# A three-layer transformer block on one core: the start, the order of the products of rows_wide, and some orders beside them

## The chip, the cores and the metric

The kernel runs on one core of a Trainium2 chip. The metric is the device time of one execution in microseconds (us). Five engines work side by side, each through its own list of instructions: TensorE (PE in the profile, its weight loads PEld), VectorE (DVE), ScalarE (ACT), GpSimd (POOL) and SyncE (SP), which here only starts transfers. They wait for each other by semaphores: `then_inc` raises one when an instruction is done, `wait_ge` holds an engine until it has a value.

## The reference, cut to what matters

Two blocks over 256 tokens of 1024 features, all in float32.

```
first_block(x, mem):
    h = rms_norm(x, g_mix);  proj = h @ w_in          # conv, sq, sk, sv, xq, three gates
    y_conv, y_sb (stick-breaking attention), y_x (attention on rms_norm(mem) @ w_mem_kv)
    merged = gate0 * y_conv + gate1 * y_sb + gate2 * y_x
    x = x + merged @ w_out
    x = x + square(relu(rms_norm(x, g_mlp) @ w_up)) @ w_down
second_block(x), two layers:
    proj = x @ w_in;  fox attention (8 heads) and retention (4 heads, rotary q and k)
    x = layernorm(alpha * x + mixed @ w_out)
    x = layernorm(alpha * x + square(relu(x @ w_ff1)) @ w_ff2)
```

## The kernel before, in words

**Products.** A float32 product is made of three products of rounded parts (type fp32r): high weights by high operand, low weights by high operand, high weights by low operand. The high part is a rounded copy that ScalarE makes, the low part is what is left of the float32 value, by VectorE. Weights come in halves of 128 x 2048 numbers (1 MB). For each half SP loads `raw` (two slots), ScalarE's `split` (L347) copies the high part to `w_hi`, VectorE's `split` (L824) puts the low part into `w_lo` (rings of four slots each), and TensorE takes the half when `lo_ready` has counted it. SP's load of a half waits until VectorE has split the half that used the slot before.

**Three ways over a half.** `rows_part` (L1479) has weights stationary and 256 tokens moving: products of 256 columns, called narrow here. `tokens_part` (L1532, L1533, L1540) has tokens stationary and 512 weight columns moving: wide products, first the four pairs with high operand, then the four with low operand. `rows_wide` (L1516, L1518), used for 14 halves in each of three feed-forward networks (`ffn`), has weights stationary and moves the high and low operand together (512 columns) under the high weights, then the high operand alone (256) under the low weights; for each of two groups `nt` it goes over eight `k`, and the two products of a `k` follow each other.

**The start.** The first two halves come in eight pieces of 512 columns. SP starts x (transposed, four pieces of 256 KB) and the eight pieces of weights by turns on its one queue. In `front_piece` ScalarE multiplies x by the gain (L569) and copies the weights' high part (L572), VectorE makes both low parts (L1137, L1143), and `front_half` on TensorE (L1732 to L1734) takes a piece when its low weights are there. Then ScalarE squares x, VectorE adds the squares (L852, L854), TensorE sums them over partitions (L1743, L1586), and from the variance come a logarithm and an exponential on ScalarE (L367, L369) and a Newton step on VectorE (L838 to L842). With this root `values_out` (L578) scales the products of halves 0 and 1, then of 2 and 3, out of PSUM, and `rms_tile` (L872), `rms_hi` (L383) and `rms_lo` (L878) make the normed operand. The orders of ScalarE and VectorE over these steps and the splits of halves 2 to 7 are written out by hand; they are in the diff. TensorE takes halves 2 and 3 with `tokens_part`, 4 and 5 with `rows_first` on the gained x, and from 6 on the normed operand, of which it waits for one quarter after the other. Half 5 needs the bank that values_out(1) reads.

**The merged half.** Before the product with `w_out` (halves WO1 = 60 to 63) the sum of the gated branches is turned by TensorE (`turn_merged`, L1566) into PSUM banks `turned(m, j)` of `aps`, copied by ScalarE (L651) and its low part made by VectorE (L1240). The banks of `j` = 1 are those that half 61 accumulates in, so half 61 waits until the low part of `j` = 1 is made (the `c = m + 3`).

**mlp_norm** adds the residual (L904), squares (L405 on ScalarE), takes the root and scales (L930, four chunks); TensorE turns a chunk (L1558, `turn`), ScalarE copies it (`turn_hi`, L390), VectorE makes the low part (`turn_lo`, L896). **The layers:** `rotate` (L1360 to L1366) turns q and k of the retention in four steps, which TensorE then transposes (`turn_rotated`, L1879). **ffn** goes in a loop of three rounds (`Fori`) over up (two halves of `rows_wide`), down (two halves of `tokens_part` for both blocks of 128 tokens), up, down; `last_down` takes the last two halves, block 0 of the tokens first. Then `layer_norm` adds (L906), takes statistics (L955) and ends in the stores of the output.

## Time and profile before

| | us |
|---|---|
| median of 3 runs (1213.28 to 1213.96) | 1213.61 |
| the profiled execution | 1213.38 |
| its span, first to last instruction | 1211.6 |

The rows of the trace that the prediction rests on stand in a section of their own. In them times are us from the span's start unless marked ns. A timeline row is: start, duration, engine, line, operation, what it writes <- what it reads, shapes, and in brackets the engine's idle time ahead of it with what ended it; `x2` means that like neighbours are merged. L12 is line 12 of the kernel before. A queue's rows end in q (SPq). Matmuls are pipelined: one row's end lies behind the next row's start, and the distance of two starts is the pace. A plain float32 product is counted as two.

### The profile page before, as it was taken

How to read it: one execution, taken by the hardware profiler on the slowest of the kernel's cores; microseconds unless marked ns; L12 is line 12 of the kernel's file. 1: busy time of each engine (PE TensorE's matmuls, PEld its weight loads, DVE VectorE, ACT ScalarE, POOL GpSimd, SP SyncE). 2: the span in 40 equal slices, each digit the busy share in tenths (PEclk: the TensorE clock that was granted, in tenths of full speed). 3: DMA queues.
4: the chain of work that ended last, by engine and by line, in shares of the span. 5: the costliest groups of instructions: out<-in, count | busy, mean ns of one | idle time of the engine just before them, and what ended most of it. 6: DMA issues, size and time to landing. Idle time of an engine off the chain costs nothing.

```text
span 1211.6 us, 16483 instructions
## 1 busy us (share of the span) xinstructions
PE 1192.4 (98%) x6488; PEld 1012.0 (84%) x6488; DVE 802.4 (66%) x951; ACT 616.2 (51%) x769; POOL 3.5 (0%) x10
## 2 busy tenths in 40 slices
PE   7999999999999999999999999999999999999997
PEld 6999988888888788888888878888878878888885
DVE  5687986564656576656368686665686768766555
ACT  6577675564445455344356545443536554544441
POOL 0000000000000000000000000000000000000000
PEclk9999999999999999999999999999999999999999
DMA  7565354543554365555264446555536444655540
GB/s 254 210 209 174 117 189 151 208 172 139 221 206 177 113 235 200 182 202 179 104 243 174 148 175 219 203 201 179 195 113 249 169 148 174 206 211 175 206 173 35
DMA packets 34488, 219.22 MB, mean 181 GB/s; under 512 B 4080, under 2 KB 6144, under 8 KB 9088
## 3 DMA queue, kind: packets, MB, share of 16 engines
q1 hardware_dynamic: 33792, 216.31, 50.4%
q0 software_dynamic: 640, 2.11, 0.5%
q8 instruction: 41, 0.67, 0.2%
q14 instruction: 15, 0.12, 0.0%
HBM read 217.34 MB, written 1.06 MB: 180 GB/s over the span
## 4 chain that ended last, share of the span: by engine, by line
PE 92%; DVE 6%; ACT 1%; issue 1%; DMA 0%; SPq 0%; DVEq 0%; ACTq 0%
PE gps L1479 13%; PE gps L1516 13%; PE gps L1532 9%; PE gps L1540 9%; PE gps L1533 9%; PE aps L1532 8%; PE aps L1533 8%; PE aps L1540 8%; PE gps L1518 7%; DVE w_lo L824 1%; PE aps L1558 1%; DVE rs L955 1%; ACT w_hi L347 1%; DVE B L965 1%; PE aps L1695 1%
## 5 line engine op out<-in xcount | busy, mean ns | idle before, releaser
L824 DVE TENSOR_TENSOR w_lo<-raw,w_hi 128x2048 fp32r<-128x2048 f32 x194 | 444.2, 2291 | 240.2 <-ACT w_hi L347 239.3
L347 ACT ACTIVATE w_hi<-raw 128x2048 fp32r<-128x2048 f32 x194 | 371.4, 1915 | 211.8 <-PE aps L1540 106.3
L1516 PE MATMUL gps<-R_both,w_hi 128*128 128x512 f32 x672 | 238.1, 399 | 0.0
L1518 PE MATMUL gps<-R_both,w_lo 128*128 128x256 f32 x672 | 188.8, 281 | 0.0
L1532 PE MATMUL aps<-w_hi,Q_hi 128*128 128x512 f32 x416 | 162.7, 391 | 0.5 <-DVE Q_lo L1240 0.5
L1533 PE MATMUL aps<-w_lo,Q_hi 128*128 128x512 f32 x416 | 162.5, 391 | 0.0
L1516 PEld LDWEIGHTS gps<-R_both,w_hi 128*128 128x128 f32 x672 | 126.4, 188 | 30.8
L1518 PEld LDWEIGHTS gps<-R_both,w_lo 128*128 128x128 f32 x672 | 127.1, 189 | 0.8
L1532 PE MATMUL gps<-w_hi,H_hi 128*128 128x512 f32 x288 | 114.9, 399 | 0.0
L1533 PE MATMUL gps<-w_lo,H_hi 128*128 128x512 f32 x288 | 112.6, 391 | 0.0
L1540 PE MATMUL aps<-w_hi,Q_lo 128*128 128x512 f32 x416 | 111.7, 391 | 0.0
L1479 PE MATMUL gps<-H_hi,w_hi 128*128 128x256 f32 x416 | 110.0, 287 | 0.0
L1479 PE MATMUL gps<-H_hi,w_lo 128*128 128x256 f32 x416 | 108.5, 283 | 0.0
L1532 PEld LDWEIGHTS aps<-w_hi,Q_hi 128*128 128x128 f32 x416 | 78.1, 188 | 17.4 <-DVE w_lo L824 0.7
L1540 PEld LDWEIGHTS aps<-w_hi,Q_lo 128*128 128x128 f32 x416 | 77.9, 188 | 16.4
L1533 PEld LDWEIGHTS aps<-w_lo,Q_hi 128*128 128x128 f32 x416 | 78.2, 188 | 15.7
L1479 PE MATMUL gps<-H_lo,w_hi 128*128 128x256 f32 x416 | 83.2, 283 | 0.0
L1479 PEld LDWEIGHTS gps<-H_hi,w_hi 128*128 128x128 f32 x416 | 79.6, 191 | 3.1 <-issue 3.0
L435 ACT ACTIVATE staged<-gps 128x256 f32<-128x256 f32 x84 | 27.6, 381 | 105.6 <-PE gps L1518 105.6
L1479 PEld LDWEIGHTS gps<-H_hi,w_lo 128*128 128x128 f32 x416 | 79.8, 192 | 0.1
L1540 PE MATMUL gps<-w_hi,H_lo 128*128 128x512 f32 x288 | 77.7, 392 | 0.0
L1532 PEld LDWEIGHTS gps<-w_hi,H_hi 128*128 128x128 f32 x288 | 54.1, 188 | 14.3 <-issue 3.5
(239 smaller groups left out, 1562.8 us busy)
## 6 DMA issues: line engine op xcount, KB each, us to landing
raw<-w SPq DMA_DIRECT2D x194, 1024.0 KB, 4.8
B<-rows SPq DMA_DIRECT2D x4, 1024.0 KB, 4.7
raw<-w SPq DMA_DIRECT2D x8, 256.0 KB, 5.7
B<-turns POOLq DMA_DIRECT2D x4, 512.0 KB, 4.6
B<-x_t SPq DMA_DIRECT2D x4, 256.0 KB, 5.3
B<-mem_t SPq DMA_DIRECT2D x1, 1024.0 KB, 8.8
B<-x SPq DMA_DIRECT2D x1, 1024.0 KB, 6.8
out<-B SPq DMA_DIRECT2D x4, 256.0 KB, 2.0
```

The source lines that it names most:

```text
L347: act.activation(w_hi[:, ring(l), :], raw[:, raw_slot(l), :], ACT.Copy)\
L435: act.activation(staged[:, a, nt * T:(nt + 1) * T], wide_bank(a, nt)[:, T:2 * T], ACT.Copy)\
L824: dve.tensor_tensor(w_lo[:, ring(l), :], raw[:, raw_slot(l), :], w_hi[:, ring(l), :].bitcast(F32), ALU.subtract)\
L955: st.mark(dve.bn_stats(stats[:, m, 6 * j:6 * j + 6], chunk(X, m, j)))
L965: dve.scalar_tensor_tensor(t, t, stats[:, m, 17:18], b_row[:, 512 * j:512 * (j + 1)], ALU.mult, ALU.add).then_inc(s["t_z"], 1)
L1479: return pe.matmul(gps[:, bank_, nt * T:(nt + 1) * T], w[:, r, c:c + P], op[:, k, :], start=start, stop=stop, skip_group_check=True)
L1516: pe.matmul(b, w_hi[:, r, c:c + P], R_both[:, k, :, :].rearrange("p i t -> p (i t)"), start=(k == 0), stop=False, skip_group_check=True)
L1518: ins = pe.matmul(b[:, 0:T], w_lo[:, r, c:c + P], R_hi[:, k, :], start=False, stop=(k == KT - 1), skip_group_check=True)
L1532: pe.matmul(out, x, w_hi[:, r, c], start=(start and k == ks[0]), stop=False)
L1533: pe.matmul(out, x, w_lo[:, r, c], start=False, stop=False)
L1540: ins = pe.matmul(out, op_lo[:, 4 * g + k, rows], w_hi[:, r, c], start=False, stop=(stop and k == ks[-1]))
L1558: ins = pe.transpose(turned(m, j)[:, k * P:(k + 1) * P], chunk(src, m, j)[:, k * P:(k + 1) * P], ident)
```

## The change

x goes through ScalarE's DMA queue, ahead of its table load, and SP starts weights alone. TensorE begins with six products of zeros, behind a memset on VectorE. `front_half` takes the high weights with both parts of x first and the low weights last, with finer waits. The orders of ScalarE and VectorE in the start, in mlp_norm and around `rotate(3)` are changed. `rows_wide` makes the eight wide products of a group first, then the eight narrow ones. The merged half's `j` = 1 is turned into banks 3 and 0 of `gps`, half 61 waits for `m + 1` alone, and ScalarE's table load there moves behind the copies. In the last ffn the loop has two rounds, the third is written out, and its last four halves go over block 0 of the tokens first, then block 1.

```diff
@@ -161,7 +161,7 @@
         raw_loaded = [sem("raw_loaded0"), sem("raw_loaded1")]
         x_piece = [sem(f"x_piece{i}") for i in range(4)]
         w_piece = [sem(f"w_piece{i}") for i in range(8)]
-        names = """qk_scaled front_g front_hi front_lo vs_var vs_log vs_scale mem_loaded x_loaded par_loaded cst_loaded con_loaded lpar_loaded out_stored
+        names = """zeros front_xlo qk_scaled front_g front_hi front_lo vs_var vs_log vs_scale mem_loaded x_loaded par_loaded cst_loaded con_loaded lpar_loaded out_stored
             hi_ready lo_ready gemm_done evac act_step dve_step pads
             nsq nsum nvar nlog nrow nt nhi nlo resid acc_ready sqsum rows_loaded gn_row_loaded
             t_sq t_var t_log t_z t_tr
@@ -201,6 +201,10 @@

             return aps[:, 2 * m + j, :]

+        def merged_turned(m, j):
+
+            return turned(m, 0) if j == 0 else (gps[:, 3, :], gps[:, 0, :])[m]
+
         def operand(buf, m, j):

             return buf[:, 4 * j:4 * j + 4, m * P:(m + 1) * P]
@@ -258,9 +262,6 @@

             sp.dma_start(par[:, :], par1).then_inc(s["par_loaded"], 16)
             for k in range(KT):
-                if k % 2 == 0:
-                    sp.dma_start(B6[:, k:k + 2, :], x_t[k * P:(k + 2) * P].rearrange("(k p) t -> p k t", p=P))\
-                      .then_inc(x_piece[k // 2], 16)
                 c = slice(k % 4 * 512, k % 4 * 512 + 512)
                 sp.dma_start(raw[:, raw_slot(k // 4), c], w1[k // 4][:, c]).then_inc(w_piece[k], 16)
             sp.dma_start(cst[:, :], con1).then_inc(s["cst_loaded"], 16)
@@ -410,9 +411,9 @@
                 root_start(0, 0)
                 turn_hi(N_MLP, 0, R_hi)
                 squared(1, 0)
-                turn_hi(N_MLP, 1, R_hi)
                 squared(1, 1)
                 root_start(0, 1)
+                turn_hi(N_MLP, 1, R_hi)
                 split(0, FFN1 + 2)
                 turn_hi(N_MLP, 2, R_hi)
                 turn_hi(N_MLP, 3, R_hi)
@@ -561,6 +562,9 @@
                                    bias=small[:, 1, 2 * h + t:2 * h + t + 1], scale=1.0 / 16,
                                    accum_out=small[:, 2, 2 * h + t:2 * h + t + 1]).then_inc(s["cx_exp"], 1)

+            for k in range(0, KT, 2):
+                act.dma_start(B6[:, k:k + 2, :], x_t[k * P:(k + 2) * P].rearrange("(k p) t -> p k t", p=P))\
+                   .then_inc(x_piece[k // 2], 16)
             act.preload_act_table_set("natural_log_exp_and_others")
             def front_piece(k):
                 c = slice(k % 4 * 512, k % 4 * 512 + 512)
@@ -592,13 +596,13 @@
             values_out(0)
             rms_hi(0, 0, B4, H_hi)
             split(0, 4)
+            split(0, 5)
+            values_out(1)
             rms_hi(0, 1, B4, H_hi)
-            split(0, 5)
             rms_hi(0, 2, B4, H_hi)
-            values_out(1)
             split(0, 6)
+            split(0, 7)
             rms_hi(0, 3, B4, H_hi)
-            split(0, 7)
             staged_n = 0
             for h in range(SQK, FFN1):
                 ps = bank(h)
@@ -642,14 +646,14 @@
                             act.wait_ge(s["staged_free"], staged_n - 1)
                             evac(staged[:, m, :], bank(h - 1 + m), h + 1)
                             staged_n += 1
-                elif h == WO1:
-                    act.preload_act_table_set("natural_log_exp_and_others")
                 if h in (GATED["conv"] + 4, WO1):
                     for m in range(2):
                         j = int(h == WO1)
                         act.wait_ge(s["mg_tr"], 2 * j + m + 1)
-                        act.activation(operand(Q_hi, m, j), four(turned(m, j)), ACT.Copy)\
+                        act.activation(operand(Q_hi, m, j), four(merged_turned(m, j)), ACT.Copy)\
                            .then_inc(s["mg_hi"], 1)
+                if h == WO1:
+                    act.preload_act_table_set("natural_log_exp_and_others")
                 if h == MEM0:

                     act.wait_ge(s["mem_loaded"], 16)
@@ -926,20 +930,25 @@
                                       EPS_RMS, ALU.add, ALU.add).then_inc(s["t_var"], 1)
                     dve.wait_ge(s["t_var"], m + 1)
                     root(0, m)
-                    for j in range(2):
-                        dve.scalar_tensor_tensor(chunk(scaled, m, j), chunk(X, m, j), stats[:, m, 17:18],
-                                                 g_mlp[:, 512 * j:512 * (j + 1)], ALU.mult, ALU.mult)\
-                           .then_inc(s["t_z"], 1)
+
+                def scaled_chunk(m, j):
+                    dve.scalar_tensor_tensor(chunk(scaled, m, j), chunk(X, m, j), stats[:, m, 17:18],
+                                             g_mlp[:, 512 * j:512 * (j + 1)], ALU.mult, ALU.mult)\
+                       .then_inc(s["t_z"], 1)

                 added(0, 0)
                 added(0, 1)
                 dve.wait_ge(s["rows_loaded"], 16)
                 rooted(0)
+                scaled_chunk(0, 0)
+                scaled_chunk(0, 1)
                 added(1, 0)
                 turn_lo(N_MLP, 0, R_hi, R_lo)
                 added(1, 1)
+                rooted(1)
+                scaled_chunk(1, 0)
                 turn_lo(N_MLP, 1, R_hi, R_lo)
-                rooted(1)
+                scaled_chunk(1, 1)
                 turn_lo(N_MLP, 2, R_hi, R_lo)
                 split(0, FFN1 + 2)
                 turn_lo(N_MLP, 3, R_hi, R_lo)
@@ -1135,7 +1144,8 @@
                 c = slice(k % 4 * 512, k % 4 * 512 + 512)
                 dve.wait_ge(s["front_g"], k + 1)
                 dve.scalar_tensor_tensor(Q_lo[:, k, :], B6[:, k, :], par[:, G_MIX + k:G_MIX + k + 1],
-                                         Q_hi[:, k, :].bitcast(F32), ALU.mult, ALU.subtract)
+                                         Q_hi[:, k, :].bitcast(F32), ALU.mult, ALU.subtract)\
+                   .then_inc(s["front_xlo"], 1)
                 if k % 4 == 3:
                     dve.wait_ge(s["hi_ready"], k // 4 + 1)
                 else:
@@ -1144,6 +1154,7 @@
                                   ALU.subtract).then_inc(s["lo_ready" if k % 4 == 3 else "front_lo"], 1)

             g_mix, g_mem = (par[:, g:g + KT] for g in (G_MIX, G_MEM))
+            dve.memset(staged[:, 0, 0:T], 0.0).then_inc(s["zeros"], 1)
             dve.wait_ge(s["par_loaded"], 16)
             for k in range(KT):
                 front_piece(k)
@@ -1169,9 +1180,9 @@
             rms_root(0)
             rms_tile(0, B6, B4, g_mix)
             split(0, 4)
+            split(0, 5)
             rms_tile(1, B6, B4, g_mix)
             rms_lo(0, 0, B4, H_hi, H_lo)
-            split(0, 5)
             rms_tile(2, B6, B4, g_mix)
             rms_lo(0, 1, B4, H_hi, H_lo)
             scaled_half(0)
@@ -1237,7 +1248,7 @@
                     for m in range(2):
                         j = int(h == WO1)
                         dve.wait_ge(s["mg_hi"], 2 * j + m + 1)
-                        dve.tensor_tensor(operand(Q_lo, m, j), four(turned(m, j)),
+                        dve.tensor_tensor(operand(Q_lo, m, j), four(merged_turned(m, j)),
                                           operand(Q_hi, m, j).bitcast(F32), ALU.subtract)\
                            .then_inc(s["mg_lo"], 1)
                 if h == MEM0:
@@ -1399,10 +1410,10 @@
                     if l == 12:
                         for h in range(RET_HEADS):
                             retention_mask(h)
+                    if l == 10:
+                        rotate(3)
                     if l <= LRV:
                         split(g0, p + l + 4)
-                    if l == 10:
-                        rotate(3)
                     if l == 12:
                         dve.wait_ge(s["gn_row_loaded"], 16 * (ly + 1))
                         scaled_gate(0)
@@ -1515,6 +1526,8 @@
                         c = k * 256 + nt * P
                         pe.matmul(b, w_hi[:, r, c:c + P], R_both[:, k, :, :].rearrange("p i t -> p (i t)"),
                                   start=(k == 0), stop=False, skip_group_check=True)
+                    for k in range(KT):
+                        c = k * 256 + nt * P
                         ins = pe.matmul(b[:, 0:T], w_lo[:, r, c:c + P], R_hi[:, k, :],
                                         start=False, stop=(k == KT - 1), skip_group_check=True)
                 ins.then_inc(s["gemm_done"], 1)
@@ -1563,7 +1576,7 @@

                 pe.wait_ge(s["mg"], 2 * j + m + 1)
                 for k in range(4):
-                    ins = pe.transpose(turned(m, j)[:, k * P:(k + 1) * P],
+                    ins = pe.transpose(merged_turned(m, j)[:, k * P:(k + 1) * P],
                                        chunk(merged, m, j)[:, k * P:(k + 1) * P], ident)
                 ins.then_inc(s["mg_tr"], 1)

@@ -1627,13 +1640,29 @@
                     ins.then_inc(s["up_tr"], 1)
                 rows_wide(h0, l0 + 3, 1)
                 down(h0, l0 + 4, 0, ub + 2, first=True)
-                with pe.Fori(0, 3) as f:
+                with pe.Fori(0, 3 if n < LAYERS else 2) as f:
                     hf, uf = h0 + f * 8, ub + f * 4
                     up(hf, l0 + 6, uf + 3)
                     down(hf, l0 + 8, 1, uf + 4)
                     up(hf, l0 + 10, uf + 5)
                     down(hf, l0 + 12, 0, uf + 6)
-                last_down(l0 + 30, 1, ub + 16)
+                if n < LAYERS:
+                    last_down(l0 + 30, 1, ub + 16)
+                    return
+                up(h0 + 16, l0 + 6, ub + 11)
+                down(h0 + 16, l0 + 8, 1, ub + 12)
+                up(h0 + 16, l0 + 10, ub + 13)
+                for m in range(2):
+                    for par_ in range(2):
+                        pe.wait_ge(s["hidden"], ub + 14 + 2 * par_)
+                        for a in range(2):
+                            l = l0 + 28 + 2 * par_ + a
+                            pe.wait_ge(s["lo_ready"], h0 + (l + 1))
+                            ins = tokens_part(l, acc(m, a), m, par_, Q_hi, Q_lo, stop=(par_ == 1))
+                            if m:
+                                ins.then_inc(s["gemm_done"], 1)
+                            elif par_:
+                                ins.then_inc(s["acc_ready"], 1)


             def sb_scores(i):
@@ -1721,19 +1750,31 @@
                 ins.then_inc(s["cx_o"], 1)

             def front_half(g):
+                def product(w, x, k, m, start=False, stop=False):
+                    return pe.matmul(gps[:, m, :], x[:, 4 * g + k, m * P:(m + 1) * P],
+                                     w[:, g, 512 * k:512 * (k + 1)], start=start, stop=stop)
+
                 for k in range(4):
+                    if k == 3:
+                        pe.wait_ge(s["hi_ready"], g + 1)
+                    else:
+                        pe.wait_ge(s["front_hi"], 3 * g + k + 1)
+                    for m in range(2):
+                        product(w_hi, Q_hi, k, m, start=(g == 0 and k == 0))
+                    pe.wait_ge(s["front_xlo"], 4 * g + k + 1)
+                    for m in range(2):
+                        product(w_hi, Q_lo, k, m)
                     if k == 3:
                         pe.wait_ge(s["lo_ready"], g + 1)
                     else:
                         pe.wait_ge(s["front_lo"], 3 * g + k + 1)
-                    c = slice(512 * k, 512 * (k + 1))
                     for m in range(2):
-                        x_hi, x_lo = (x[:, 4 * g + k, m * P:(m + 1) * P] for x in (Q_hi, Q_lo))
-                        pe.matmul(gps[:, m, :], x_hi, w_hi[:, g, c], start=(g == 0 and k == 0), stop=False)
-                        pe.matmul(gps[:, m, :], x_hi, w_lo[:, g, c], start=False, stop=False)
-                        ins = pe.matmul(gps[:, m, :], x_lo, w_hi[:, g, c], start=False, stop=(g == 1 and k == 3))
+                        ins = product(w_lo, Q_hi, k, m, stop=(g == 1 and k == 3))
                 ins.then_inc(s["gemm_done"], 1)

+            pe.wait_ge(s["zeros"], 1)
+            for _ in range(6):
+                pe.matmul(aps[:, 0, 0:T], staged[:, 0, 0:P], staged[:, 0, 0:T], start=True, stop=True)
             for g in range(2):
                 front_half(g)
             pe.wait_ge(s["cst_loaded"], 16)
@@ -1786,9 +1827,8 @@
                 elif h < WO1 + 2:
                     pe.wait_ge(s["lo_ready"], h + 1)
                     for m in range(2):
-                        c = m + 1 if h == WO1 else m + 3
                         ins = tokens_part(h, acc(m, h - WO1), m, 0, Q_hi, Q_lo, start=True,
-                                          hi_ready=(s["mg_lo"], c))
+                                          hi_ready=(s["mg_lo"], m + 1))
                         if m == 1:
                             ins.then_inc(s["gemm_done"], 1)
                         if h == WO1:
```

## Rows read from the trace of the kernel before

**Rows 1.** Page, first part: busy us (share) and instructions by engine.
```profile
PE 1192.4 (98%) x6488; PEld 1012.0 (84%) x6488; DVE 802.4 (66%) x951; ACT 616.2 (51%) x769; POOL 3.5 (0%) x10
```

**Rows 2.** Waits of TensorE: line <- releaser: us in total, times, longest.
```profile
PE gps L1479 <- ACT B L578: 1.5, 1, 1.5
PE aps L1879 <- DVE B L1366: 0.7, 2, 0.4
PE aps L1558 <- DVE B L930: 0.6, 1, 0.6
PE aps L1532 <- DVE Q_lo L1240: 0.5, 1, 0.5
```

**Rows 3.** TensorE's timeline: narrow run, pairs of rows_wide, wide products behind each.
```profile
617.72 0.28 PE L1479 MATMUL gps<-H_hi,w_hi 128*128 128x256 f32 x1
...
619.88 0.40 PE L1532 MATMUL gps<-w_hi,H_hi 128*128 128x512 f32 x1
...
621.72 1.07 PE L1540 MATMUL gps<-w_hi,H_lo 128*128 128x512 f32 x4
...
1169.98 0.40 PE L1516 MATMUL gps<-R_both,w_hi 128*128 128x512 f32 x1
...
1175.28 0.40 PE L1516 MATMUL gps<-R_both,w_hi 128*128 128x512 f32 x1
...
1180.93 0.40 PE L1532 MATMUL aps<-w_hi,Q_hi 128*128 128x512 f32 x1
...
1182.80 1.08 PE L1540 MATMUL aps<-w_hi,Q_lo 128*128 128x512 f32 x4
```

**Rows 4.** Timeline of the end: VectorE, TensorE, VectorE.
```profile
1186.07 2.29 DVE L824 TENSOR_TENSOR w_lo<-raw,w_hi 128x2048 fp32r<-128x2048 f32 x1 [1.11 <-ACT w_hi L347]
...
1201.85 1.07 PE L1540 MATMUL aps<-w_hi,Q_lo 128*128 128x512 f32 x4
...
1203.97 0.67 DVE L906 SCALAR_TENSOR_TENSOR B<-B,aps 128x512 f32<-128x512 f32 x1
```

**Rows 5.** TensorE's timeline: first products to the start of half 4.
```profile
6.67 0.79 PE L1732 MATMUL gps<-w_hi,Q_hi 128*128 128x512 f32 x1 [6.67 <-DVE w_lo L1143]
...
12.38 0.53 PE L1733 MATMUL gps<-w_lo,Q_hi 128*128 128x512 f32 x1
...
20.49 0.95 PE L1743 MATMUL aps<-cst,B 128*128 128x1 f32 x8
21.30 1.11 PE L1586 MATMUL aps<-B,cst 128*128 128x256 f32 x4
...
33.17 0.32 PE L1479 MATMUL gps<-Q_hi,w_hi 128*128 128x256 f32 x1
```

**Rows 6.** Lines view of TensorE, plain float32 product: count, busy us, mean ns.
```profile
L1695 PE MATMUL aps<-B 128*128 128x256 f32 x32 | 7.6, 380 | 0.0
```

**Rows 7.** VectorE's timeline: splits of halves 2, 3 and 4.
```profile
18.60 2.29 DVE L824 TENSOR_TENSOR w_lo<-raw,w_hi 128x2048 fp32r<-128x2048 f32 x1 [0.46 <-ACT w_hi L347]
...
23.73 2.29 DVE L824 TENSOR_TENSOR w_lo<-raw,w_hi 128x2048 fp32r<-128x2048 f32 x1
...
30.69 2.29 DVE L824 TENSOR_TENSOR w_lo<-raw,w_hi 128x2048 fp32r<-128x2048 f32 x1 [2.50 <-ACT w_hi L347]
```

**Rows 8.** ScalarE's timeline: first x, late piece, split 3, first logarithm.
```profile
4.15 0.51 ACT L569 ACTIVATE Q_hi<-B,par 128x256 fp32r<-128x256 f32 x1 [2.12 <-DMA B<-x_t]
...
12.70 0.63 ACT L572 ACTIVATE w_hi<-raw 128x512 fp32r<-128x512 f32 x1 [0.19 <-DMA raw<-w]
...
20.02 1.91 ACT L347 ACTIVATE w_hi<-raw 128x2048 fp32r<-128x2048 f32 x1 [1.46 <-DMA raw<-w]
22.71 0.20 ACT L367 ACTIVATE small<-small 128x2 f32<-128x2 f32 x1 [0.77 <-DVE small L1154]
```

**Rows 9.** SP's queue, timeline: first x, last two pieces of weights.
```profile
1.20 0.42 SPq L262 DMA_DIRECT2D B<-x_t  x1
...
6.47 1.32 SPq L265 DMA_DIRECT2D raw<-w  x2
```

## The prediction, made before the changed kernel was run

> **What bounds the kernel now.** I read the page's first part, then TensorE's waits, then the timeline where the diff works. The first part shows TensorE busy for 1192.4 us, 98% of the span, with VectorE at 66% and ScalarE at 51% [rows 1]. The reader is to see that nothing but TensorE's own pace and its few idle places can give time. The waits name those places [rows 2], besides the start: 1.5 us behind ScalarE's values_out, 0.7 us in two places behind rotate, 0.6 us behind mlp_norm's scaled chunk, 0.5 us behind the low part of the merged half. A listed wait costs more than its row: a wide product (512 columns) is 0.40 us long, yet the next starts 0.227 us later (92 starts from 1180.93 to 1201.85 take 20.92 us [rows 3, 4]), so 0.17 us of overlap is lost with each wait. The sum is made against the profiled execution, 1213.38 us (span 1211.6 and 1.8 around it); the median of the runs, 1213.61, lies 0.23 above. A measurement of this kernel can tell about 0.2%, 2.4 us, from no change.
>
> **The change, part by part.**
>
> *Start, up to half 3.* The first product starts at 6.67, released by the first low part of the weights [rows 5]. Thirteen starts from 6.67 to 12.38 take 5.71 us, 0.44 each, against 0.227 later: these are the two levels of the clock, 1.2 and 2.4 GHz, and it rose near 12.4 after TensorE had been at work since 6.67. The six products of zeros begin after a memset on an idle VectorE, near 1.2. Each is a plain-f32 product that the trace counts twice (16 in the program for the 32 of L1695, 0.24 us busy each at the high level [rows 6]); at the low level I take twice that, 12 x 0.43 = 5.2 us, so they end near 6.4. The memset is not in these rows; I bound it by 0 and by half a 128x512 operation, under 0.4 us. The high part of a piece is there ahead of the low one by VectorE's operation, a quarter of the 2.29 of a whole half [rows 7] or 0.6 us, so the first true product would start near 6.4 when the zeros end. If the clock then rises near 7, the 48 products at 0.227 (10.9 us) end near 17.6 and not 20.5, where the small sums follow [rows 5]. That gain is not kept whole. Next the sums of squares need VectorE's addition, which is done at 18.14 (18.60 less the 0.46 idle [rows 7]), and take 1.9 us (20.49 to 21.30 + 1.11 [rows 5]), so 20.1. VectorE then is in the split of half 2 until 20.89, and ScalarE in that of half 3 until 21.93, where before it stood idle for 0.77 us waiting for the variance [rows 8]. So the logarithm starts at 21.93 and not 22.71, and the chain behind it (Newton step, split 3, root, tile, high copy, split 4, which ended at 30.69 + 2.29 = 32.98 [rows 7]) comes 0.78 us sooner. TensorE began half 4 at 33.17 [rows 5], 0.19 after that split; now it will wait for it, and starts at 32.25: **0.9 us**. So of some 2.7 us gained on TensorE 1.8 are given back at half 4.
>
> *x through ScalarE's queue.* SP's issues of x take 0.42 each or more, and the last two pieces of weights are issued from 6.47 on [rows 9]; without x these come some 2 us sooner. ScalarE pays four issues ahead of its table load, 1.7 us, out of the 2.12 us that it waits for x [rows 8]; if that cover goes, the front starts up to 1.7 us late. What is gained is bounded by the transfers: at piece 6 ScalarE waited 0.19 us for a landing, and otherwise worked through. Ends: 0.75 us sooner for half 3's load, if ScalarE alone sets the pace, to 0.3 later, if x shares the bandwidth that w had. I take **0.2**, near the row of 0.19. The Trainium skill's page "DMA: Bandwidth & Descriptors", in "Issuing engines are not separate DMA queues", says that transfers started by different engines run on the same 16 DMA engines, and that only the issue time is saved. By that rule this term would be 0 and the time 0.2 us higher; SP's rows show that the issues are the shorter part.
>
> *values_out ahead of rms_hi.* In the new order values_out(1) follows split 5 and no longer three norm copies that wait for VectorE's tiles. Half 3 ends by 32.25, and split 5 needs a load that is issued when split 3 ends, at 25.2; with 6 us allowed for it and 1.9 for the split, values_out(1) starts near 33.3, over 4 us before half 5 asks for it: the 1.5 goes, with its overlap **1.7 us**. Next late would be half 6: its split now stands behind tile 1, tile 2 and two low parts; by the same durations it ends about 0.5 us before TensorE asks. If that cover fails it costs up to 0.5.
>
> *rows_wide grouped.* Now a wide and a narrow product alternate. Fifteen pairs from 1169.98 to 1175.28 take 5.30 us: 0.353 a pair [rows 3]. Narrow ones alone take 0.120 (18 from 617.72 to 619.88). Eight wide ones take 1.84 behind a run of narrow ones (619.88 to 621.72) and 1.87 behind pairs (1180.93 to 1182.80). A group of eight wide and eight narrow is then 1.84 + 0.96 = 2.80 against 2.827, 0.027 us less; there are 2 groups in 42 halves: 84 x 0.027 = **2.3 us**. The 21 places where down follows get the 1.84 for the 1.87: 21 x 0.026 = **0.55**. Ends: 1.87 in each group makes it nothing; the steady 0.227 makes it 84 x 0.05 = 4.2.
>
> *Merged half.* With its second half turned into banks of gps, WO1 + 1 needs no low part of it: 0.5 + 0.17, **0.7 us**. The table load moves behind the copies on ScalarE, ahead of the split of half 64; TensorE comes to that half only after the four remaining parts of WO1, which hides it.
>
> *mlp_norm.* The scaled chunk that the third turn waits for moves ahead of two operations on VectorE, and its root ahead of a copy on ScalarE. The wait of 0.6 goes, **0.7 us** with its overlap and less 0.06, by which the copy now behind the root may come late.
>
> *rotate(3)* goes ahead of a split that is wanted three halves later; the split is some 2.2 us later under that cover. Both waits go: 0.7 + 2 x 0.17, **1.0 us**.
>
> *Last ffn.* TensorE now ends all of the first 128 tokens before the others. Its last product ended at 1202.92, but the last addition on VectorE started at 1203.97, as the norm of the first tokens was in its way [rows 4]. That norm now starts 5.4 us (24 products) sooner, so the addition follows the product: **1.0 us**. Added demand: the last half's low part (1186.07 + 2.29 = 1188.36) is wanted 36 products behind 1180.93, at 1189.1; 0.7 in hand.
>
> Sum: 0.9 + 0.2 + 1.7 + 2.3 + 0.55 + 0.7 + 0.7 + 1.0 + 1.0 = 9.05. 1213.38 - 9.05 = **1204.3 us**.
>
> **The rivals.**
> 1. *Grouping gives nothing.* Eight wide products after only eight narrow ones may stay at 1.87, as behind pairs. For it: the slow pace holds for the first eight wide ones, which is the whole group. Against it: 1.84 behind the narrow run [rows 3]. Without 2.85 us: 1207.1. Chance 0.17.
> 2. *The start gives little.* ScalarE's issues or x's share of the bandwidth hold the weights back, or the clock rises late, and half 4 begins where it did; or half 6 becomes late. The order of values_out still gives 1.7. Without 1.1 and with 0.5 at half 6: 1205.9; if the start is 2 us late besides, 1207.9. For it: a late piece was still waited for, 0.19 us [rows 8], so x that comes sooner can hold weights back. Against it: ScalarE's 2.12 us of idle time there. Chance 0.15.
> 3. *The gains are taken back further on.* VectorE's and ScalarE's chains would then be as tight as TensorE, and the waits come back at the next halves. For it: half 4 shows it, and 0.5 and 0.7 us of slack are thin. Against it: no other wait is in the list. With 2.4 us or less left: 1211 to 1213.6, no change to be told. Chance 0.04.
> 4. *Slower: narrow products in a run are paced by something that the wide ones now hide*, in rows_wide alone. Each 0.01 us over 0.120 costs 672 x 0.01 = 6.7 us. With the other terms (6.2) the kernel is slower than before once a narrow one takes more than 0.133; at 0.15 it is 1213.4 - 6.2 + 17.9 = 1225. Against it: the 0.120 of the narrow run of [rows 3], with the same tiles for weights. Chance 0.03.
>
> **How the numbers follow.** The forecast has 0.61, its own range 1202.5 to 1206. The range of 8 in 10 takes in rivals 1 and 2 and the better end of grouping (1.9 more) with the better end of the landings: 1201.3 to 1207.9. Faster by over 0.2%: forecast and rivals 1 and 2, 0.93. Within 0.2%: rival 3, 0.04. Slower: rival 4, 0.03.
>
> **What would show it.** First true products near 6.4, 0.44 apart for a few and then 0.227; half 4's first product waiting on a split of VectorE, near 32.2; no row of L578, of rotate or of the merged low part in TensorE's waits; eight wide products of rows_wide in 1.84 and narrow ones 0.12 apart; the last addition 0.04 us behind TensorE's last product. The forecast is wrong if the 32 pairs of two halves still take 32 x 0.353 = 11.3 us, or if a new wait of over 1 us stands on TensorE.

## The result, and the profile after

The changed kernel takes **1204.12 us** (median of 6 runs, 1203.70 to 1204.34), the kernel before beside it 1213.96: a ratio of 0.9919, with a 95% interval of 0.9906 to 0.9931. The profiled execution took 1204.25 us, 1202.4 of it span. The forecast was 1204.3.

First the page's first part and then TensorE's waits (released line <- releaser: us in total, times, longest), both of the changed kernel, to be held against [rows 1] and [rows 2]:

```profile
PE 1191.9 (99%) x6500; PEld 1013.8 (84%) x6500; DVE 802.5 (67%) x952; ACT 616.0 (51%) x769; POOL 3.5 (0%) x10
```

```profile
PE aps L1777 <- DVE staged L1157: 1.2, 1, 1.2
PE aps L1571 <- DVE B L974: 0.4, 2, 0.2
PE aps L1784 <- DVE B L858: 0.3, 1, 0.3
PE gps L1545 <- ACT B L582: 0.2, 1, 0.2
PE gps L1754 <- ACT w_hi L576: 0.2, 1, 0.2
PE gps L1545 <- DVE w_lo L828: 0.2, 1, 0.2
```

The four waits of [rows 2] are gone: values_out (1.5 us), rotate (0.7), mlp_norm (0.6) and the merged half's low part (0.5). What is left is the wait for the memset and places of 0.2 or 0.3 us.

The start, TensorE's timeline of the changed kernel, to be held against [rows 5]:

```profile
1.20 5.42 PE L1777 MATMUL aps<-staged 128*128 128x256 f32 x12 [1.20 <-DVE staged L1157]
6.42 0.73 PE L1754 MATMUL gps<-w_hi,Q_hi 128*128 128x512 f32 x2
...
17.62 0.61 PE L1754 MATMUL gps<-w_lo,Q_hi 128*128 128x512 f32 x2
18.52 1.02 PE L1784 MATMUL aps<-cst,B 128*128 128x1 f32 x8 [0.29 <-DVE B L858]
...
20.68 0.50 PE L1545 MATMUL gps<-w_hi,Q_hi 128*128 128x512 f32 x1 [0.17 <-DVE w_lo L828]
...
32.53 0.36 PE L1490 MATMUL gps<-Q_hi,w_hi 128*128 128x256 f32 x1
```

The zeros fill 1.20 to 6.42, the first true products follow at 6.42 and the front ends 2.4 us sooner than before. The small sums then start 1.97 us sooner, half 4 only 0.64 (32.53 for 33.17). It waits behind these steps of ScalarE and VectorE (same kernel, their timelines, against [rows 7, 8]):

```profile
20.31 1.92 ACT L348 ACTIVATE w_hi<-raw 128x2048 fp32r<-128x2048 f32 x1 [2.01 <-DMA raw<-w]
22.13 0.18 ACT L368 ACTIVATE small<-small 128x2 f32<-128x2 f32 x1
```

```profile
30.09 2.29 DVE L828 TENSOR_TENSOR w_lo<-raw,w_hi 128x2048 fp32r<-128x2048 f32 x1 [2.50 <-ACT w_hi L348]
```

Split 3 now waits 2.01 us for its load, and the logarithm stands behind it; VectorE's split 4 ends at 30.09 + 2.29 = 32.38, and half 4 starts 0.15 later.

rows_wide and the end, TensorE's timeline, then VectorE's last additions, of the changed kernel, against [rows 3, 4]:

```profile
1161.62 1.98 PE L1527 MATMUL gps<-R_both,w_hi 128*128 128x512 f32 x8
1163.43 1.12 PE L1531 MATMUL gps<-R_both,w_lo 128*128 128x256 f32 x8
1164.38 2.00 PE L1527 MATMUL gps<-R_both,w_hi 128*128 128x512 f32 x8
1166.22 1.11 PE L1531 MATMUL gps<-R_both,w_lo 128*128 128x256 f32 x8
...
1193.64 1.07 PE L1553 MATMUL aps<-w_hi,Q_lo 128*128 128x512 f32 x4
```

```profile
1194.75 0.69 DVE L910 SCALAR_TENSOR_TENSOR B<-B,aps 128x512 f32<-128x512 f32 x1 [1.30 <-PE aps L1553]
```

Eight wide products take 1.81 us behind other wide ones (1161.62 to 1163.43) and 1.84 behind narrow ones (1164.38 to 1166.22); eight narrow ones take 0.95. The last addition waits for TensorE now. TensorE's last four products start at 1193.64, the last of them at 1194.32; before, that one started at 1202.53 (the last of the four of [rows 4]), so TensorE's list ends 8.2 us sooner, and the span 9.2.

### The profile page after: what moved, and what is told of

The parts are those of the page before. It is cut to its first block, busy times and chain, and to the rows that moved or that the text cites. A ratio compares the mean times of both kernels' runs of the same rounds, so it can differ in the third digit from the quotient of the medians.

```text
span 1202.4 us, 16502 instructions
## 1 busy us (share of the span) xinstructions
PE 1191.9 (99%) x6500; PEld 1013.8 (84%) x6500; DVE 802.5 (67%) x952; ACT 616.0 (51%) x769; POOL 3.5 (0%) x10
## 4 chain that ended last, share of the span: by engine, by line
PE 92%; DVE 4%; DMA 2%; ACT 1%; issue 1%; SPq 0%; DVEq 0%; ACTq 0%
PE gps L1527 13%; PE gps L1490 12%; PE gps L1545 10%; PE gps L1553 10%; PE gps L1546 10%; PE aps L1546 8%; PE aps L1545 8%; PE aps L1553 8%; PE gps L1531 7%; DMA raw<-w 2%; ACT w_hi L348 1%; DVE w_lo L828 1%; PE aps L1571 1%; PE aps L1724 1%; PE aps L1748 1%
## 5 line engine op out<-in xcount | busy, mean ns | idle before, releaser
L1527 PE MATMUL gps<-R_both,w_hi 128*128 128x512 f32 x672 | 167.9, 392 | 0.0
L1527 PEld LDWEIGHTS gps<-R_both,w_hi 128*128 128x128 f32 x672 | 122.1, 189 | 22.8
L1531 PEld LDWEIGHTS gps<-R_both,w_lo 128*128 128x128 f32 x672 | 91.7, 190 | 6.6
L1531 PE MATMUL gps<-R_both,w_lo 128*128 128x256 f32 x672 | 93.7, 282 | 0.0
```

The costliest lines, as they stand in the source:

```text
L1527: pe.matmul(b, w_hi[:, r, c:c + P], R_both[:, k, :, :].rearrange("p i t -> p (i t)"), start=(k == 0), stop=False, skip_group_check=True)
L1531: ins = pe.matmul(b[:, 0:T], w_lo[:, r, c:c + P], R_hi[:, k, :], start=False, stop=(k == KT - 1), skip_group_check=True)
```

## The experiments

Shifts are of TensorE's matching products between two traces. A landing is when a load's last packet is in.

### Grouping alone, and undone

e1_group_alone gives this edit to the kernel before; e2_pairs_back takes it from the changed kernel.

```diff
                     for k in range(KT):
                         c = k * 256 + nt * P
                         pe.matmul(b, w_hi[:, r, c:c + P], R_both[:, k, :, :].rearrange("p i t -> p (i t)"),
                                   start=(k == 0), stop=False, skip_group_check=True)
+                    for k in range(KT):
+                        c = k * 256 + nt * P
                         ins = pe.matmul(b[:, 0:T], w_lo[:, r, c:c + P], R_hi[:, k, :],
```

> The kernel before, with rows_wide grouped and nothing else. Theory A, that a wide product is paced slower when narrow ones stand before it, and grouping leaves fewer such places: 1213.9 less 3.5 us (672 pairs in 234.3 us and not 237.1, and 21 down halves sooner by 0.03 each), so near 1210.4; the waits at values_out (1.5 us), rotate and mlp_norm stay. Theory B, that the stretches of the ffn became shorter because of what surrounds them (waits that the other edits removed, transfers): no change, within 0.5 us of the kernel before.

> The changed kernel with the pairs of rows_wide restored. Theory A: 3.5 us slower than the changed kernel, 1207.6, with wide-to-narrow 236 ns and narrow-to-wide 117 ns again. Theory B: within 0.5 us of the changed kernel's 1204.1.

Measured: e1 1210.05 us (1209.50 to 1210.97) beside 1213.58 for the kernel before, ratio 0.9972 [0.9961, 0.9982], 3.5 us; e2 1207.41, 3.3 above the changed kernel. The changed kernel did not run beside e2; its two medians, 1204.12 and 1203.95, stand for it here and below. Theory A in both. From the start stamps of all 1344 products of rows_wide: 237.1 us before, 234.3 in e1 and in the changed kernel, 237.3 in e2; the 21 down halves (`tokens_part`) that follow a group gain 0.03 each. e1 keeps the four waits of [rows 2]:

```profile
PE gps L1479 <- ACT B L578: 1.5, 1, 1.5
PE aps L1881 <- DVE B L1366: 0.7, 2, 0.4
PE aps L1560 <- DVE B L930: 0.6, 1, 0.6
PE aps L1534 <- DVE Q_lo L1240: 0.5, 1, 0.5
```

### Groups of 16 and of 4

e7_groups_of_16 makes the wide products of both `nt` first; e8_groups_of_4 cuts each group in two.

```diff
                 for nt in range(2):
                     b = wide_bank(a, nt)
                     for k in range(KT):
...
+                for nt in range(2):
+                    b = wide_bank(a, nt)
                     for k in range(KT):
                         c = k * 256 + nt * P
                         ins = pe.matmul(b[:, 0:T], w_lo[:, r, c:c + P], R_hi[:, k, :],
```

```diff
                 for nt in range(2):
                     b = wide_bank(a, nt)
-                    for k in range(KT):
+                    for kk in range(0, KT, 4):
+                        for k in range(kk, kk + 4):
...
-                    for k in range(KT):
+                        for k in range(kk, kk + 4):
...
```

> The changed kernel with 16 wide products, for both nt, and then 16 narrow ones. Theory A, a cost of 0.02 us at each return from narrow to wide: 42 returns fewer, 0.9 us off, 1203.2. Theory B, that the gain came with the grouping whatever the size of a group: no change, 1204.1.

> The changed kernel with groups of four wide and four narrow products. Theory A: 84 returns more at 0.02 us, 1.7 us slower, 1205.8. Theory B: no change, 1204.1.

TensorE's timeline of e7, then of e8:

```profile
1160.38 3.79 PE L1527 MATMUL gps<-R_both,w_hi 128*128 128x512 f32 x16
1164.00 2.08 PE L1533 MATMUL gps<-R_both,w_lo 128*128 128x256 f32 x16
1165.91 3.82 PE L1527 MATMUL gps<-R_both,w_hi 128*128 128x512 f32 x16
1169.57 2.08 PE L1533 MATMUL gps<-R_both,w_lo 128*128 128x256 f32 x16
```

```profile
1163.61 1.07 PE L1528 MATMUL gps<-R_both,w_hi 128*128 128x512 f32 x4
1164.51 0.64 PE L1532 MATMUL gps<-R_both,w_lo 128*128 128x256 f32 x4
1164.98 1.09 PE L1528 MATMUL gps<-R_both,w_hi 128*128 128x512 f32 x4
1165.91 0.63 PE L1532 MATMUL gps<-R_both,w_lo 128*128 128x256 f32 x4
```

By the means over all places of these traces, a run of wide products takes longer behind narrow ones than behind wide ones: 0.022 us for 4 (0.929 for 0.907), 0.028 for 8 (1.841 for 1.813), 0.027 for 16 (3.654 for 3.627), and 0.009 for a single one in the kernel before (0.236 for 0.227). So the price comes with the return and stops growing within the first eight products, and fewer returns make the sum smaller: rows_wide takes 233.4 us in e7, 234.3 in groups of 8, 235.4 in e8. The times are 1203.68 and 1205.92. Theory A has the mechanism, and its 0.9 us for e7 is what TensorE's stamps show; the times show 0.3 to 0.4, within the spread of the runs. e8's 1.8 looks like theory A's 1.7, but rows_wide gives only 1.1 of it: in its profiled execution half 4 started 0.9 later, behind a late load (below), and what made its other runs slow was not traced.

### The start: x on SP's queue, and no zeros

```diff
 e3_x_on_sp
             for k in range(KT):
+                if k % 2 == 0:
+                    sp.dma_start(B6[:, k:k + 2, :], ...).then_inc(x_piece[k // 2], 16)
-            for k in range(0, KT, 2):
-                act.dma_start(B6[:, k:k + 2, :], ...).then_inc(x_piece[k // 2], 16)
 e4_no_zeros
-            dve.memset(staged[:, 0, 0:T], 0.0).then_inc(s["zeros"], 1)
-            pe.wait_ge(s["zeros"], 1)
-            for _ in range(6):
-                pe.matmul(aps[:, 0, 0:T], staged[:, 0, 0:P], staged[:, 0, 0:T], start=True, stop=True)
```

> The changed kernel with x back on SP's queue, between the weight pieces, as before the change. Theory A, that the four issues on ScalarE put 1 MB of x into the transfers ahead of the weights, which then land later: the last weight piece lands as in the kernel before the change or a little sooner and the load of half 3 near 20.0 and not 20.29, so half 4 starts 0.2 to 0.4 us sooner than the changed kernel's 32.53; 1203.8. Theory B, that of the prediction, that SP's issue time is saved on ScalarE's queue: half 4 starts 0.2 us later, 32.7; 1204.3. Theory C, that landings at the start differ by more from one execution to the next than the queue makes: half 4 anywhere from 32.3 to 33.5 whatever the queue, no rule to be told.

> The changed kernel without the memset and the six products of zeros. Theory A, that the zeros bring the clock to its high level sooner and half 4's chain hands on only a part of it: the first product at 6.3, products 0.44 apart up to about 12, the front's last product near 20.0 and not 17.84, but half 4 only 0.4 to 0.9 us later than 32.53; 1204.5 to 1205.0. Theory B, that half 4 is set by the landing of half 3's load alone: front as in A, half 4 at 32.5, 1204.1. Theory C, that everything gained at the front is kept: 2.2 us later, 1206.3.

Measured: e3 1204.57 us (1204.06 to 1205.27), half 4 at 32.77; e4 1203.67 (1203.44 to 1204.78), half 4 at 33.49 in the profiled execution, the longest of the four, whose transfers came late. So e4 is compared with e8, which has the zeros and whose transfers came as late. Split 3 on ScalarE and the start of half 4 on TensorE, first of e4, then of e8:

```profile
19.71 0.95 PE L1780 MATMUL aps<-cst,B 128*128 128x1 f32 x8
...
21.29 1.92 ACT L348 ACTIVATE w_hi<-raw 128x2048 fp32r<-128x2048 f32 x1 [1.98 <-DMA raw<-w]
...
33.49 0.36 PE L1489 MATMUL gps<-Q_hi,w_hi 128*128 128x256 f32 x1
```

```profile
21.24 1.92 ACT L348 ACTIVATE w_hi<-raw 128x2048 fp32r<-128x2048 f32 x1 [2.07 <-DMA raw<-w]
...
33.46 0.36 PE L1490 MATMUL gps<-Q_hi,w_hi 128*128 128x256 f32 x1
```

With and without zeros half 4 starts 12.2 us after split 3 has its load: theory B of e4, in its mechanism and in its median. In e3 theory A fell: its last weight piece landed at 14.00, not sooner than the changed kernel's 13.07. The sign is that of the prediction (theory B): half 4 0.24 later, the median 0.45 or 0.62 above the changed kernel's two, the ranges overlapping. But over all profiles half 3's load landed from 20.00 to 20.89 in three executions with x on SP's queue and from 19.98 to 21.26 in nine with x on ScalarE's, where halves 2 and 3 were loaded as in the changed kernel: theory C, and the queue's own share stays open.

### The old order of the front's products

```diff
 e13_old_front_order (and without the zeros, as e4)
+                    pe.wait_ge(s["front_lo"], 3 * g + k + 1)
                     for m in range(2):
                         product(w_hi, Q_hi, k, m, ...)
+                        product(w_lo, Q_hi, k, m)
+                        ins = product(w_hi, Q_lo, k, m, ...)
```

> The changed kernel without the zeros and with the front's products in their old order (each piece's low weights awaited first). Theory A, that half 4 starts at the later of half 3's landing plus 12.24 us and the small sums' start plus 12.67 us: the sums start at 20.2 to 20.6, half 4 at 32.9 to 33.3 (later only if the landing is past 20.9), 1204.7; so the order of the front's products gives 0.5 us and the zeros, on top of it, nothing. Theory B, that landing alone decides: half 4 at 32.5, 1204.1.

> The changed kernel once more, beside the others. If the 0.4 us that it lost at the first transposes of layer 0 in its first profile came from that execution's landings: TensorE's products there stand 0.4 us sooner against the ones ahead of them; if from the change itself, they stand where they stood. 1204.1 in both.

Measured: e13 1204.05 us (1203.46 to 1204.82), the changed kernel beside it (e12_after_again) 1203.95 (1203.67 to 1204.15). Half 4 starts at 32.39 in both. e13, TensorE, ScalarE and TensorE:

```profile
7.07 0.79 PE L1753 MATMUL gps<-w_hi,Q_hi 128*128 128x512 f32 x1 [7.07 <-DVE w_lo L1153]
...
19.71 0.28 PE L1773 MATMUL aps<-cst,B 128*128 128x1 f32 x2
...
20.00 1.91 ACT L348 ACTIVATE w_hi<-raw 128x2048 fp32r<-128x2048 f32 x1 [2.01 <-DMA raw<-w]
...
32.39 0.32 PE L1489 MATMUL gps<-Q_hi,w_hi 128*128 128x256 f32 x1
```

The rule of theory A holds (the later of the load of half 3 + 12.2 and the sums + 12.67; both constants were read off earlier runs, so the rows of e13 and e12 test them). Its input was wrong: the sums came at 19.71 and not at 20.2 to 20.6, so that half 4 and the time came out as theory B said (32.5 and 1204.1).

| execution | split 3 starts + 12.22 | sums start + 12.67 | half 4 |
|---|---|---|---|
| before | 32.24 | **33.16** | 33.17 |
| e1 (front as before) | 33.14 | **33.26** | 33.26 |
| e13 (old order, no zeros) | 32.22 | **32.38** | 32.39 |
| e4 (new order, no zeros) | **33.51** | 32.38 | 33.49 |
| changed kernel | **32.53** | 31.19 | 32.53 |
| changed kernel again | **32.39** | 31.11 | 32.39 |
| e3 (x on SP) | **32.78** | 31.61 | 32.77 |
| e8 | **33.46** | 32.14 | 33.46 |

e2, e5 and e7 start half 4 at 32.48, 32.53 and 32.33, within 0.01 us of the load's term; of the runs with these loads e6 alone starts it later than both terms (34.90), as its half 2 came late (last section). Of the 2 us by which the zeros and the order bring the sums forward, at most the first 0.9 could ever count, and in e13 0.78 of it came without them, since its products went over to the faster pace early (below). Whether x's queue or chance made that so is open. By the table, in an execution that stays at the slow pace as long as before did, the zeros and the order would be worth up to those 0.8 (an estimate); in the medians (1204.05 without, 1203.95 with) they are worth nothing that shows.

### The order of values_out, and the later edits

e5_old_values_order puts back both engines' old orders for halves 4 to 7; e6_late_parts_undone takes back the merged half, mlp_norm, rotate(3) and the last ffn.

```diff
 e5: ScalarE
             split(0, 4)
+            rms_hi(0, 1, B4, H_hi)
             split(0, 5)
-            values_out(1)
-            rms_hi(0, 1, B4, H_hi)
             rms_hi(0, 2, B4, H_hi)
+            values_out(1)
 e6: VectorE, one of four
                     if l <= LRV:
                         split(g0, p + l + 4)
+                    if l == 10:
+                        rotate(3)
```

> The changed kernel with ScalarE's and VectorE's old order for halves 4 to 7 (values_out(1) behind two norm copies, split 5 behind tile 1). Theory A, that the order removes the wait: a wait of 1.5 us on values_out(1) ahead of half 5 is back, 1.7 us slower, 1205.8. Theory B, that the wait shrank because the start is sooner: wait of 0.6 us or less, within 0.7 of 1204.1.

> The changed kernel with four later edits undone at once, each read at its own place: the merged half, mlp_norm, rotate(3) and the last ffn. Theory A, that each gain is local and kept to the end: 0.8, 0.8, 1.2 (two layers) and 1.0 us come back at these places and stay, 1207.9. Theory B, that an edit's gain is taken back by the next chain when the others are there: under 2.5 us in all, below 1206.6, and the shift of TensorE's products against the changed kernel shrinks between the places.

Measured: e5 1205.77 us (1205.39 to 1206.21), with this row of TensorE ahead of half 5:

```profile
40.05 0.39 PE L1490 MATMUL gps<-Q_hi,w_hi 128*128 128x256 f32 x1 [1.53 <-ACT B L582]
```

Its shift against the changed kernel is 0.0 at half 4, 1.69 at the first product behind this wait and 1.79 from the next on. e6: 1207.39 us (1207.21 to 1209.94, the profiled execution being the longest, with a late load at its start that the last section shows). Three of the waits of [rows 2] are back in it:

```profile
PE aps L1904 <- DVE B L1377: 0.7, 2, 0.4
PE aps L1571 <- DVE B L935: 0.6, 1, 0.6
PE aps L1545 <- DVE Q_lo L1251: 0.5, 1, 0.5
```

The shift grows by 0.77 at the merged half, 0.81 at mlp_norm, 0.58 and 0.59 at the two places of rotate, and the end behind TensorE's last product by 0.99. Against the second profile of the changed kernel (e12_after_again) nothing of it shrinks in between; against the first it shrinks by 0.36 at the start of layer 0, where that profile itself lost time (rival 3 below). Theory A in both.

### Loading halves 2 and 3 early

If half 3's load sets half 4's start, taking that load off the chain must free it. B1 and B2 are not used until half 4 is done, so e10_early_loads loads halves 2 and 3 there without waiting for a split, and puts split 4 ahead of a norm copy that waits for VectorE. e11_early_and_16 adds the groups of 16.

```diff
-            load(0, 2, w1[2])
-            load(0, 3, w1[3])
-            load(0, 4, w1[4])
-            load(0, 5, w1[5])
+            for l in (2, 3):
+                sp.dma_start(early(l), w1[l]).then_inc(raw_loaded[l % 2], 16)
+            for l in (4, 5):
+                sp.wait_ge(s["lo_ready"], l - 3)
+                sp.wait_ge(raw_loaded[l % 2], 16)
+                sp.dma_start(raw[:, l % 2, :], w1[l]).then_inc(raw_loaded[l % 2], 16)
...
             values_out(0)
+            split(0, 4)
             rms_hi(0, 0, B4, H_hi)
-            split(0, 4)
```

> The changed kernel with halves 2 and 3 loaded at the start into two buffers that are free then (so neither load waits for a split), and ScalarE's split 4 ahead of its first norm copy. Theory A, that half 4's start was the landing of half 3's load plus 12.24 us: with that load landed before 18.5, TensorE works through halves 2 and 3 (four parts of 2.72 us behind a start near 20.6), half 4 starts at 31.6 to 31.9 and not 32.53, and the 0.7 to 0.9 us are kept: 1203.4. Theory B, that the early loads take bandwidth from the first weights and x: the last piece lands 0.5 us or more later, half 2 starts after 21.2, half 4 at 32.3 or later, 1204 or more. Theory C, that it is given back at half 5 or 6 (their splits or the norm copies): half 4 at 31.8, but half 7 within 0.2 us of the changed kernel's.

> Early loads and groups of 16 together. Theory A, that the two add: 0.8 at the start and 0.9 in rows_wide, 1202.5. Theory B, that what the start gains is lost at a later transfer: 1203.2.

Split 3 on ScalarE and half 4 on TensorE, of e10:

```profile
18.71 1.91 ACT L354 ACTIVATE w_hi<-B 128x2048 fp32r<-128x2048 f32 x1 [0.55 <-DMA B<-w]
...
31.56 0.28 PE L1496 MATMUL gps<-Q_hi,w_hi 128*128 128x256 f32 x1
```

Measured: e10 1202.89 us (1202.58 to 1203.73), e11 **1202.39** (1201.98 to 1202.78), beside 1203.95 for the changed kernel (1203.67 to 1204.15). Half 4 starts at 31.56 with no wait ahead of it, 0.98 sooner than in the changed kernel's first profile and 0.84 sooner than in its second, and the shift is still there at 600 us. Theory A in both, with e10's time 0.5 below the one it gave. The early loads and the moved split 4 were not run apart. e11 is 1.6 us under the changed kernel, and their ranges don't meet; it beats both kernels.

## Why the prediction was right, and where it was not

1204.3 was forecast and 1204.12 measured, but the sum hides errors of either sign. Gains in us, by shifts of TensorE's products against the kernel before (the start's at the first product of half 4, the others' as they stand behind the place, the last ffn's by the end behind the products); the last column is the experiment that undid a step or made it alone.

| step | forecast | changed kernel, two profiles | taken back or alone |
|---|---|---|---|
| start and x, at half 4 | 0.9 + 0.2 | 0.63, 0.77 | zeros and order: 0 in these executions (e4, e13) |
| values_out | 1.7 | 1.79, 1.79 | 1.79 (e5) |
| rows_wide, with the down halves | 2.85 | 3.4, 3.4 | 3.5, 3.3 (e1, e2) |
| merged half | 0.7 | 0.77, 0.77 | 0.77 (e6) |
| mlp_norm | 0.7 | 0.81, 0.81 | 0.81 (e6) |
| rotate(3), two layers | 1.0 | 1.2, 1.2 | 1.17 (e6) |
| last ffn | 1.0 | 0.97, 0.96 | 0.99 (e6) |

The first profile's gains add to some 9.5 us, and 0.4 of that is lost again in layer 0 (rival 3), which leaves the 9.1 between the two profiled executions. That the forecast's 9.05 meets this is in part luck: the start and x gave some 0.4 less than was forecast, rows_wide 0.6 and the local waits 0.4 more, and the loss in layer 0 was not forecast.

- *Start.* Right that half 4 would wait for split 4 and that most of the front's gain would be given back there (0.63 and 0.77 for 0.9). What failed is the step that let the zeros carry it. The prediction had the row for it: ScalarE "stood idle for 0.77 us waiting for the variance" is all that sooner sums can give, so 0.8 us of the 2.4 would have done, and that came without zeros too (e13). From there half 3's load is the limit, a wait that the prediction's sum did not have: split 3 waited 2.01 us for it, and the chain behind it starts with it. e10 shows what lay behind it: one more microsecond.
- *x through ScalarE's queue.* The 0.2 is not borne out: split 3 began at 20.31 and 20.17, not before the 20.02 of [rows 8]. In the changed kernel's profile the load of half 3 landed 0.29 us later than before, the bad end of the bound. The prediction's reading of ScalarE, that it waited for a landing at piece 6 "and otherwise worked through", was wrong: in the kernel before it also waited 0.61, 0.54 and 0.45 us for the first three pieces of weights. In the changed kernel x's last piece landed sooner (10.29 for 11.98) but the third piece of weights later (9.07 for 8.52), and from that piece on VectorE works without idle time. First ScalarE at the third piece, then VectorE's last low part of half 1, of the changed kernel, and VectorE's of the kernel before:

```profile
9.10 0.63 ACT L576 ACTIVATE w_hi<-raw 128x512 fp32r<-128x512 f32 x1 [0.85 <-DMA raw<-w]
```

```profile
14.79 0.68 DVE L1153 TENSOR_TENSOR w_lo<-raw,w_hi 128x512 fp32r<-128x512 f32 x1
```

```profile
14.37 0.69 DVE L1143 TENSOR_TENSOR w_lo<-raw,w_hi 128x512 fp32r<-128x512 f32 x1
```

Half 3's load waits for this step. So sooner landings of the last pieces (13.07 for 13.34) bought nothing: in the nine executions with x on ScalarE's queue the load is issued 6.4 to 6.6 us behind the landing of the third piece, in the three with x on SP's queue 1.74 or 1.75 behind that of the last, and it takes 4.7 to 5.2 us. By the Trainium skill's page "DMA: Bandwidth & Descriptors", section "Issuing engines are not separate DMA queues", the term would be 0; with landings 1.3 us apart between executions of one arrangement, no run here tells 0 from 0.2.
- *values_out.* Right, and half 6's split, of which 0.5 us was said to be left, was not waited for.
- *rows_wide.* The mechanism was right, its size was 0.6 too small. The eight wide products behind narrow ones do take 1.84, but in 21 of the 84 groups the wide run stands behind other wide ones and takes 1.81 (in three it stands behind transposes and takes 1.92), and eight narrow ones take 0.95, not 0.96. Each of the 21 down halves gains 0.031 and not 0.026, since the gain goes on a little behind the eighth product. Rival 1 (1.87 in each group) falls with e1 and e2, rival 4 with 0.119 us a narrow product in a run.
- *Merged half, mlp_norm, rotate, last ffn.* Right, to 0.2 us each: a wait's row plus 0.17 of lost overlap comes 0.04 to 0.13 short of what each wait gave back.
- *Rival 3*, gains taken back further on, seemed to show once: the first profile lost 0.42 us at the first transposes of layer 0. ScalarE's splits there, of the changed kernel and then of e12, which is the same kernel again:

```profile
627.38 1.92 ACT L348 ACTIVATE w_hi<-raw 128x2048 fp32r<-128x2048 f32 x1 [6.00 <-DMA raw<-w]
```

```profile
626.11 1.92 ACT L348 ACTIVATE w_hi<-raw 128x2048 fp32r<-128x2048 f32 x1 [3.61 <-DMA raw<-w]
```

The same load came 1.3 us sooner in the second execution, and there nothing is lost. So the loss comes and goes with that transfer, in one and the same kernel. It is not a thing of one execution, though: of the ten other runs that build on the changed kernel five (e2, e7, e8, e10, e11) lose 0.1 to 0.25 us at this place, and the kernel before and e1 lose nothing. Rival 3 was right to that extent, and whether the change makes the late transfer more likely is open.

## What to carry to other kernels

Before pricing an engine's earlier finish, find the next thing its successor waits for: here the sums came 2 us sooner, but only 0.6 to 0.8 of it reached half 4, because a load that waits for a free slot came later than they did; loading into buffers that are idle at the start, with one split moved forward, gave a microsecond more. Where products of two widths alternate, the return to the wide ones has a price, so longer runs are better: here groups of eight gave 3.4 us, and groups of 16 another 0.9 of TensorE's time, of which the run times show 0.3 to 0.5. A wait on a pipelined engine costs its row plus the overlap that it breaks, and gains of that kind add up over a kernel when each is local.

## What was not expected of the hardware

**The pace at the start.** Products of 512 columns start 0.43 us apart at first and then 0.227, and the moment differs: without zeros there were 13 slow ones in the profile of before, 12 in e1, 10 in e4 and 7 in e13, with the first product between 6.08 and 7.08. So how much the zeros save is a matter of the execution. The Trainium skill's page "TensorE: Matmul & The Clock Gate", section "What's actually happening", says that such counts vary from run to run of one kernel; the kernel before and e1, which have the same start, differ by one, and the others have other starts. The prediction called this the clock's two levels, and the trace bears it out. Its record of the granted clock begins with the change of pace, at 12.67 in the kernel before, 12.39 in e1, 11.14 in e4, 10.53 in e13 and 6.42 in the changed kernel, where the zeros end, and it reads 1.00 from there; ahead of it there is no record, and the 1.00 that the column below shows there stands for none. In e6, whose load of half 2 came late, a wait of 2.13 us up to 22.30 was followed by the same 0.43 us pace, and there the clock is on record, at 0.50 from 22.67 to 26.09. Stretches of the kernel before at the start and then of e6 (us; busy us and count of PE, PEld, DVE, ACT, POOL; granted clock as a share, DMA share, GB/s), and e6's products:

```profile
9.00:11.00 2.00, 2.00 (x6) 1.62 (x5) 1.79 (x4) 1.95 (x5) 0.00 (x0) 1.00 0.97 316
```

```profile
22.00:24.00 2.00, 1.70 (x5) 1.37 (x6) 1.77 (x7) 1.92 (x6) 0.00 (x0) 0.67 0.32 70
24.00:26.00 2.00, 2.00 (x6) 1.54 (x5) 1.99 (x2) 0.83 (x2) 0.00 (x0) 0.50 0.95 393
26.00:28.00 2.00, 2.00 (x10) 1.66 (x9) 1.73 (x4) 0.14 (x1) 0.00 (x0) 0.98 0.77 213
```

```profile
22.30 0.50 PE L1545 MATMUL gps<-w_hi,Q_hi 128*128 128x512 f32 x1 [2.13 <-DVE w_lo L828]
22.64 0.59 PE L1546 MATMUL gps<-w_lo,Q_hi 128*128 128x512 f32 x1
```

Both have six products in 2 us, the one ahead of its record, the other at a recorded 0.50 (1.2 of 2.4 GHz): the slow pace of the start is that of the lower level. The late load cost e6 1.6 us at the start of half 2 and 3.2 by the end of its first part: the slower clock added some 1.6.

**Wide after narrow.** Five wide products behind a narrow run start 233, 236, 228, 232 and 231 ns apart, the next 227 (means over 60 places). Why the return costs this is not shown by any run.
